# Modulation tiles add into one PSUM bank through zero-padded conditions, and the two gate tiles of the latent projections become one

## The chip, the cores and the metric

The kernel runs on one core of one Trainium2 chip. The metric is the device time of one launch in microseconds, the median of three runs. All arithmetic is in float32. The host only lays the inputs out.

## The reference

Two transformer blocks over 256 latent tokens of width 1024, with 256 memory or context tokens beside them. The first block mixes three attentions and a feed-forward layer of 16384 small experts, of which every token gathers 128 rows. The second block has two layers, an mLSTM mixer and a retention mixer, each followed by 16 experts of three 1024 x 1024 matrices with 32 tokens each. What the change touches is the modulation: two condition vectors (one for the latent tokens, one for the context) go through SiLU and, for each layer, a 1024 x 6144 matrix, and give shifts, scales and gates for every channel:

```python
def modulate(h, shift, scale):
    return h * (1 + scale) + shift

g = p[..., 2 * nq + 2 * nv:].astype(f32)
ig = g[..., :2 * A_HEADS].reshape(bn, t, 2, A_HEADS) + ig_b.astype(f32)
lf = jax.nn.log_sigmoid(g[..., 2 * A_HEADS:].reshape(bn, t, 2, A_HEADS) + fg_b.astype(f32))
```

The second part gives the mLSTM's 16 input gates and 16 forget gates per token, from the last 32 columns of its input matrix.

## The kernel before, in words

The program is a row of stages; within one, each engine has its own list of instructions, and at the end of each block of lists all engines wait for one another. Weights come by SyncE's DMAs of 2 MB each into a ring of six places (`issue`, line 257); a place is loaded again when the matmuls that read it are done (`k.release`). The order in each list is written out by hand.

**Modulations** (class at line 553). The two matrices make 24 tiles of 512 columns. For a tile, `tensor` (line 604) multiplies the two condition columns (`k.cond`, stationary, 2 columns for each of 8 chunks of 128 channels) with the 512 columns of the weights: the 8 products go to four groups of partitions (0, 32, 64, 96) of one PSUM bank, two into each, so rows 0 and 1 of each group hold partial sums. ScalarE copies the whole bank to SBUF (`scalar`, line 569, L574). `turn_rows` (line 594, L600) then multiplies each 128 columns of the copy (stationary) with `k.pick[:, 0:2]`, which adds the four groups and puts the channels on partitions. `tensor` begins with the turn of the tile before it. Once all tiles of a span are turned, VectorE adds the bias (`vector_end`, L589). Tiles 0 to 3 run beside the peer experts, 4 to 12 in the latent scan (`latent_scan`, between the 16 units of the scan), 13 to 15 in the norm ahead of the retention's projections, 16 to 18 in the retention heads, 19 to 21 ahead of the retention's output, 22 and 23 in the norm ahead of the second layer's experts.

**Latent projections** (`latent_scan`, run by `gemm`, line 450). The tile list begins with two tiles of 16 output rows, input and forget gates, each with its 8 chunks, then 8 tiles of queries and keys and 8 of values and outputs. ScalarE empties each into SBUF and adds the gates' bias (L2066).

**Latent scan.** For each of 16 units (8 heads, 2 directions) PE makes row maxima (L1512) and, once a head, scores (L1505), VectorE the exponents (L1552), ScalarE the exponential (L1530), GpSimd the mask (L1540), VectorE the weights (L1562), PE the output (L1524), VectorE its normalisation.

**Experts** (`experts`, line 2367). Ten places of 2 MB hold expert weights: the six of the ring and four more (`WeightsAhead.load`, line 2362, L2363), filled before the experts begin. After routing, GpSimd gathers the token rows of the first experts by an indirect DMA (`fetch_rows`, L2424), and PE turns them (L2592) and begins (L2584). Every place freed is loaded again (L2547). The last of the four extra loads waits in SyncE's list until the router's matmuls (L2445) have read the buffer it overwrites.

Of the kernel before, what the change touches and what calls it, by code (L numbers as in the profile page):

```python
# [19 lines left out]
ALU = mybir.AluOpType  # L20
# [3 lines left out]
P = 128  # L24
# [12 lines left out]
NEG = -1e30  # L37
ROOT_K, ROOT_A, ROOT_B = 0.3752449290315803, -3.335382431293894, 5.000310737319491
# [81 lines left out]
class Tile:  # L120


    def __init__(self, pairs, n, load, m, row, dst, gate, bias, s, c, needs):
# [16 lines left out]
def setup(nc, ctx, dram):  # L140
# [159 lines left out]
def constants(k):  # L300
# [7 lines left out]
    with nc.Block(no_gpsimd_drain=True) as block:  # L308
# [7 lines left out]
        def _(pool):  # L316
# [15 lines left out]
            st(pool, pool.tensor_tensor(k.pick[:], k.ident[:, 0:EXPERTS], k.ident[:, 32:32 + EXPERTS], ALU.add))  # L332
            st(pool, pool.tensor_tensor(k.pick[:], k.pick[:], k.ident[:, 64:64 + EXPERTS], ALU.add))
            st(pool, pool.tensor_tensor(k.pick[:], k.pick[:], k.ident[:, 96:96 + EXPERTS], ALU.add))
# [115 lines left out]
def gemm(k, name, tiles, evac, upto, engine="act", banks=4, beside=None, between=None, behind=None,  # L450
# [29 lines left out]
    with nc.Block(no_gpsimd_drain=True) as block:  # L480
        @block.tensor
        def _(pe):
            seen = None
            for i, t in enumerate(tiles):
# [7 lines left out]
                for j, (lhsT, rhs) in enumerate(t.pairs):  # L492
                    last = pe.matmul(bank(i), lhsT, rhs, start=(j == 0), stop=(j == len(t.pairs) - 1))  # L493
# [44 lines left out]
def tile(pairs, n, load=None, m=P, row=0, dst=None, gate=None, bias=None, s=None, c=None, needs=None):  # L538
    return Tile(pairs, n, load, m, row, dst, gate, bias, s, c, needs)
# [13 lines left out]
class Modulations:  # L553
# [7 lines left out]
    def __init__(self, k, at, first, last, banks, turned):  # L561

        self.k, self.first, self.last, self.banks, self.out = k, first, last, banks, turned
        self.sc, self.pick = k.cond[:], k.pick[:, 0:2]
# [15 lines left out]
    def vector_end(self, dve, first=None, last=None):  # L580
        k = self.k
        first, last = first or self.first, last or self.last
        dve.wait_ge(self.turned, last - self.first)
        for layer in range(2):
            n0, n1 = (4 * min(max(a - 12 * layer, 0), 12) for a in (first, last))
            if n0 < n1:
                at = 2 * (48 * layer + n0 - 4 * self.first)
                bias = k.col("ada_b")[:, 48 * layer + n0:48 * layer + n1]
                k.step_v.after(dve, dve.tensor_tensor(  # L589
# [14 lines left out]
    def tensor(self, pe, a, follows=True):  # L604
# [4 lines left out]
        elif follows:  # L609
            self.turn_rows(pe, a - 1)  # L610
# [2576 lines left out]
```

## Time and profile before

| | us |
|---|---|
| median of 3 runs | 2859.63 |
| lowest and highest | 2857.07, 2861.63 |
| profiled execution, own time | 2877.04 |
| its span, first to last instruction | 2875.3 |
| PE matmul busy | 2171.1 (76%) |
| VectorE busy | 1336.9 (46%) |
| GpSimd busy | 809.1 (28%) |
| ScalarE busy | 434.5 (15%) |
| moved by DMA | 976.00 MB, mean 339 GB/s |

The busy shares are averages over stages with different limits: peer experts until 1326 us, latent norm, projections and scan to 1514, output to 1590, first layer's experts to 2086, retention to 2365, second layer's experts to 2865. A row of the timeline gives the start, the time from the first to the last of merged instructions, the engine (PEld is PE's weight load, SPq and POOLq are lists of SyncE and GpSimd), the line, the operation, the operands and the count; in brackets stands how long the engine was idle before and what ended that. One float32 product appears as two matmul records.

### The profile page before, as it was taken

The numbers are of one execution on the slowest core, as the hardware profiler recorded it, in microseconds if no ns is written. First come the engines' busy times: TensorE is split into PE (matmuls) and PEld (weight loads), VectorE is DVE, ScalarE is ACT, GpSimd is POOL, SyncE is SP. The second block draws the span as 40 slices with busy tenths as digits, with TensorE's granted clock in tenths as the row PEclk, the third lists the DMA queues.
The fourth block names the chain that finished last, engine by engine and source line by source line (L and its number), as shares of the span: only waits on it lengthen the run. The fifth ranks groups of instructions, "written<-read, shape, count | busy, mean of one in ns | idle before, by whom it ended". The sixth has DMA issues, their size and how long they took to land. (4 is left out here: it accounts for less than half of the span.)

```text
span 2875.3 us, 26014 instructions
## 1 busy us (share of the span) xinstructions
PE 2171.1 (76%) x9844; PEld 1057.4 (37%) x9844; DVE 1336.9 (46%) x2870; ACT 434.5 (15%) x932; POOL 809.1 (28%) x902
## 2 busy tenths in 40 slices
PE   8976897868747656657999699988889986655554
PEld 5544344725312222224574233322245553222222
DVE  3578344979996777774483222112231332101011
ACT  1332100112210211102122210001021221000000
POOL 3335433458777777772010000000000000000000
PEclk9985898979978777788999899999999997788887
DMA  9989999899999999996564799999962469999997
GB/s 364 401 293 370 404 409 346 313 358 393 376 363 367 381 347 368 362 399 247 187 215 160 291 409 409 409 409 409 405 248 88 142 242 364 409 409 409 409 409 287
DMA packets 297103, 976.00 MB, mean 339 GB/s; under 512 B 22673, under 2 KB 23825, under 8 KB 296849
## 3 DMA queue, kind: packets, MB, share of 16 engines
q1 hardware_dynamic: 182770, 562.20, 50.5%
q0 software_dynamic: 114208, 412.14, 37.8%
q8 instruction: 78, 1.28, 0.2%
q14 instruction: 47, 0.39, 0.0%
HBM read 902.97 MB, written 71.30 MB: 339 GB/s over the span
## 5 line engine op out<-in xcount | busy, mean ns | idle before, releaser
L2584 PE MATMUL ps<-big 128*32 128x256 f32 (+1 forms) x4608 | 585.8, 517 | 210.6 <-DMA big<-in_moe_w_up_dram 78.7
L493 PE MATMUL ps<-big 128*128 128x512 f32 (+3 forms) x1648 | 543.5, 490 | 25.7 <-ACT big L2016 7.9
L1942 PE MATMUL ps<-big 128*128 128x512 f32 x512 | 326.0, 779 | 212.1 <-ACT big L1960 100.7
L2584 PEld LDWEIGHTS ps<-big 128*32 128x32 f32 (+1 forms) x4608 | 219.9, 133 | 557.4 <-issue 261.1
L493 PEld LDWEIGHTS ps<-big 128*128 128x128 f32 (+1 forms) x1648 | 306.0, 193 | 249.0 <-issue 218.4
L1994 DVE SCALAR_TENSOR_TENSOR big<-big 128x1024 f32<-128x1024 f32 x256 | 313.6, 1226 | 97.9 <-DMA big<-peer_rows,big 82.4
L1893 POOL DMA_INDIRECT big<-in_peer_v_dram,big x256 | 297.5, 1162 | 129.8 <-issue 73.2
L1886 POOL DMA_INDIRECT big<-peer_rows,big x256 | 282.5, 1103 | 98.9 <-issue 75.0
L1942 PEld LDWEIGHTS ps<-big 128*128 128x128 f32 x512 | 114.8, 242 | 387.7 <-issue 259.4
L2696 DVE TENSOR_TENSOR big<-big,ps 128x512 f32<-128x512 f32 (+1 forms) x32 | 17.8, 555 | 471.7 <-issue 452.1
L659 POOL DMA_DIRECT2D peer_rows<-big x256 | 149.6, 592 | 288.6 <-DVE big L671 288.2
L671 DVE STREAM_TRANSPOSE big<-big 128x1024 f32<-128x1024 f32 x128 | 150.7, 1220 | 104.9 <-DMA big<-in_peer_u_t_dram 104.2
L2677 DVE TENSOR_TENSOR big<-ps,big 32x256 f32<-32x256 f32 (+1 forms) x96 | 48.9, 510 | 270.7 <-PE ps L2584 268.7
L2424 POOL DMA_INDIRECT big<-m_rows,small x12 | 11.5, 956 | 575.8 <-PE ps L2592 539.9
L1982 DVE SCALAR_TENSOR_TENSOR big<-big 128x1024 f32<-128x1024 f32 x128 | 164.1, 1282 | 14.4 <-DMA big<-in_peer_v_dram,big 12.9
L2652 ACT ACTIVATE big<-ps 128x512 f32<-128x512 f32 (+1 forms) x32 | 15.7, 490 | 552.4 <-PE ps L2584 552.4
L2625 PE MATMUL ps<-big 128*128 128x512 f32 x160 | 83.2, 660 | 19.7 <-DVE big L2677 19.7
L1716 PE MATMUL ps<-big 128*128 128x512 f32 (+2 forms) x288 | 92.9, 476 | 0.0
L1154 PE MATMUL ps<-big 128*128 128x512 f32 x192 | 87.1, 607 | 5.9 <-PEq L480 5.9
L1524 PE MATMUL ps<-big 128*128 128x129 f32 x320 | 50.3, 311 | 43.8 <-DVE big L1562 25.1
L429 POOL DMA_DIRECT2D m_rows<-big x2 | 1.2, 576 | 259.5 <-DVE big L368 259.4
L616 PE MATMUL ps<-big,cond 128*2 128x512 f32 x384 | 52.9, 674 | 26.4 <-DMA big<-in_ada_w_dram 18.0
(378 smaller groups left out, 2032.7 us busy)
## 6 DMA issues: line engine op xcount, KB each, us to landing
big<-in_moe_w_gate_dram SPq DMA_DIRECT2D x64, 2048.0 KB, 24.0
big<-in_moe_w_up_dram SPq DMA_DIRECT2D x64, 2048.0 KB, 24.0
big<-in_moe_w_down_dram SPq DMA_DIRECT2D x64, 2048.0 KB, 24.0
big<-in_peer_u_t_dram POOLq DMA_DIRECT2D x64, 1024.0 KB, 14.0
peer_rows<-big POOLq DMA_DIRECT2D x256, 256.0 KB, 8.5
big<-in_ada_w_dram SPq DMA_DIRECT2D x24, 2048.0 KB, 8.0
big<-in_mlstm_w_in_dram SPq DMA_DIRECT2D x12, 2048.0 KB, 15.4
big<-in_w_in_dram SPq DMA_DIRECT2D x8, 2048.0 KB, 19.6
```

What stands on the lines that cost most here:

```text
L493: last = pe.matmul(bank(i), lhsT, rhs, start=(j == 0), stop=(j == len(t.pairs) - 1))
L659: pool.dma_start(self.out[q][:, 8 * m:8 * m + 8], self.dst[m % self.OUT][32 * q:32 * q + 32] .rearrange("p j i c w -> p (j i) (c w)")).the ...
L671: dve.transpose(self.dst[m % self.OUT][:, j].rearrange("p i c w -> p c i w"), self.src[m % self.IN][:, j])\
L1154: pe.matmul(k.ps[:, i % 4, :], k.ht[:, c, t * P:(t + 1) * P], w[:, c, :], start=(c == 0), stop=False)
L1716: last = pe.matmul(self.bank(i), lhsT, rhs, start=(j == 0), stop=(j == len(t.pairs) - 1))
L1886: pool.indirect_dma_start(out=u_buf[n % NU], out_offset=None, in_=rows.rows, in_offset=bass.IndirectOffsetOnAxis(ap=index_of(0, n), axis=0))\
L1893: pool.indirect_dma_start(out=v_buf[n % NV], out_offset=None, in_=values, in_offset=bass.IndirectOffsetOnAxis(ap=index_of(1, n), axis=0))\
L1942: last = pe.matmul(k.ps[:, 4 + 2 * t + half, :], diag[n // 2 % 4], v_buf[n % NV][:, 512 * half:512 * half + 512], start=(n < PER and n % G ...
L1982: dve.scalar_tensor_tensor(out=x, in0=v_buf[n % NV], scalar=w[:, n:n + 1], in1=x, op0=ALU.mult, op1=ALU.add)\
L1994: dve.scalar_tensor_tensor(out=u, in0=u, scalar=1.0, in1=h2[:, t].rearrange("p q c w -> p (q c w)"), op0=ALU.mult, op1=ALU.mult, accum_out ...
L2584: last = pe.matmul(k.ps[q * M:q * M + M, bank, 0:W], lhsT(kc), w4[i % RING][:, c, q * W:q * W + W], start=(kc == 0), stop=(kc == C - 1), s ...
L2625: pe.matmul(k.ps[:, 4 + j % 2, :], wb[:, t * P:(t + 1) * P], ys[:, 512 * nh:512 * nh + 512], start=True, stop=True).then_inc(c_full, 1)
```

## The change

Three edits. **Groups of modulation tiles.** `k.cond_at` holds, for each of 8 chunks, 34 columns of zeros with the two conditions in columns 16 and 17. A window of 2n columns that starts at 16 - 2i puts the conditions in columns 2i and 2i + 1 and zeros elsewhere, so tile i of a group of n adds its two rows to the bank and zeros to the other rows. ScalarE copies the bank and PE turns it once for each group. The groups are tiles 4 to 12, 13 to 15, 16 to 18, 19 to 21, and 22 with 23; tiles 0 to 3 stay alone. **Gate tiles.** One tile whose 16 products go alternately to partitions 0 and 32 of one bank; both ScalarE copies follow it. **Experts.** For the second layer the last extra load waits until the first gather has landed, instead of for the router's matmuls.

```diff
-    k.pick = sb("pick", [P, EXPERTS])
+    k.pick = sb("pick", [P, 32])
     k.cond = sb("cond", [P, 2 * C])
+    k.cond_at = sb("cond_at", [P, C * WIDE])
...
                 for j, (lhsT, rhs) in enumerate(t.pairs):
-                    last = pe.matmul(bank(i), lhsT, rhs, start=(j == 0), stop=(j == len(t.pairs) - 1))
+                    row = 32 * (j % t.groups)
+                    last = pe.matmul(bank(i) if t.groups == 1 else k.ps[row:row + t.m, i % banks, 0:t.n], lhsT, rhs,
+                                     start=(j < t.groups), stop=(j >= len(t.pairs) - t.groups),
+                                     skip_group_check=t.groups > 1)
...
     def scalar(self, act, a):
-        i = a - self.first
-        act.wait_ge(self.full, i + 1)
-        if i >= 2:
-            act.wait_ge(self.turned, i - 1)
-        act.activation(self.res[i % 2], self.k.ps[:, self.banks[i % len(self.banks)], :], ACT.Copy).then_inc(self.kept, 1)
+        g = self.group_of[a]
+        if a != self.groups[g][-1]:
+            return
+        act.wait_ge(self.full, a - self.first + 1)
+        if g >= 2:
+            act.wait_ge(self.turned, g - 1)
+        act.activation(self.res[g % 2], self.k.ps[:, self.banks[g % len(self.banks)], :], ACT.Copy).then_inc(self.kept, 1)
...
     def turn_rows(self, pe, a):
-        i = a - self.first
-        pe.wait_ge(self.kept, i + 1)
+        g = self.group_of[a]
+        tiles = self.groups[g]
+        at, n = 8 * (tiles[0] - self.first), len(tiles)
+        pe.wait_ge(self.kept, g + 1)
         for b in range(4):
-            at = 2 * (4 * i + b)
-            last = pe.matmul(self.out[:, at:at + 2], self.res[i % 2][:, b * P:(b + 1) * P], self.pick,
-                             start=True, stop=True)
+            last = pe.matmul(self.out[:, at + 2 * n * b:at + 2 * n * b + 2 * n], self.res[g % 2][:, b * P:(b + 1) * P],
+                             self.k.pick[:, 0:2 * n], start=True, stop=True)
         last.then_inc(self.turned, 1)
...
     def tensor(self, pe, a, follows=True):
-        i = a - self.first
+        g = self.group_of[a]
+        tiles = self.groups[g]
+        i, width = a - tiles[0], 2 * len(tiles)
         if i == 0:
-            pe.wait_ge(self.done, len(self.banks))
-        elif follows:
-            self.turn_rows(pe, a - 1)
+            if g == 0:
+                pe.wait_ge(self.done, len(self.banks))
+            elif follows:
+                self.turn_rows(pe, a - 1)
...
-            last = pe.matmul(k.ps[q:q + 2, self.banks[i % len(self.banks)], :], self.sc[:, 2 * c:2 * c + 2], w[:, c, :],
-                             start=(c < 4), stop=(c >= 4), skip_group_check=True)
+            last = pe.matmul(k.ps[q:q + width, self.banks[g % len(self.banks)], :],
+                             self.sc[:, c, WIDE_AT - 2 * i:WIDE_AT - 2 * i + width], w[:, c, :],
+                             start=(i == 0 and c < 4), stop=(i == len(tiles) - 1 and c >= 4), skip_group_check=True)
...
+        k.step_v.after(dve, dve.memset(k.cond_at[:], 0.0))
         k.step_v.after(dve, dve.tensor_tensor(k.cond[:], k.cond[:], k.col("cvec"), ALU.mult))
+        k.step_v.after(dve, dve.tensor_copy(
+            k.cond_at[:].rearrange("p (c w) -> p c w", w=WIDE)[:, :, WIDE_AT:WIDE_AT + 2],
+            k.cond[:].rearrange("p (c s) -> p c s", s=2)))
...
-    for a in range(2):
-        tiles.append(tile([(w[:, c, 16 * a:16 * a + 16], ht[:, c, :]) for c in range(C)], T, g0, m=16,
-                          dst=(scan.ig, scan.fg)[a], bias=k.col(("ig_b", "fg_b")[a])[0:16, :]))
+    tiles.append(tile([(w[:, c, 16 * a:16 * a + 16], ht[:, c, :]) for c in range(C) for a in range(2)], T, g0, m=16,
+                      groups=2))
...
         if t.m == 16:
-            return eng.activation(t.dst, ps, ACT.Identity, bias=t.bias)
+            eng.activation(scan.ig, ps, ACT.Identity, bias=k.col("ig_b")[0:16, :])
+            return eng.activation(scan.fg, k.ps[32:48, 0, 0:T], ACT.Identity, bias=k.col("fg_b")[0:16, :])
...
                 if s == X - 1:
-                    sp.wait_ge(by_expert, 1)
+                    sp.wait_ge(*((by_expert, 1) if S > 1 else (gathered, 16)))
                 ahead.load(sp, s)
```

`vector_end` now adds the bias in one instruction for each group and layer, from the order in which a group's turn leaves the channels; beside the peer experts these are four instructions, and they were one. `k.pick` grows from 16 to 32 columns.

## Rows read from the trace of the kernel before

**Rows 1.** The page: what DMA moved in 40 equal slices of the span.

```profile
GB/s 364 401 293 370 404 409 346 313 358 393 376 363 367 381 347 368 362 399 247 187 215 160 291 409 409 409 409 409 405 248 88 142 242 364 409 409 409 409 409 287
```

**Rows 2.** Windows: length, busy of PE, PEld, DVE, ACT, POOL, PEclk, DMA share, GB/s.

```profile
1347.00:1430.00 83.00, 82.96 (x260) 48.41 (x258) 36.28 (x112) 17.38 (x33) 0.00 (x0) 1.00 0.48 170
1451.39:1460.69 9.30, 9.30 (x65) 6.49 (x64) 7.86 (x29) 2.38 (x3) 2.52 (x6) 1.00 0.65 228
...
2289.30:2304.50 15.20, 15.20 (x121) 11.71 (x120) 8.57 (x16) 6.71 (x23) 0.00 (x0) 1.00 0.95 336
...
2366.00:2396.00 30.00, 11.63 (x94) 6.83 (x86) 13.92 (x50) 6.80 (x16) 2.14 (x3) 0.72 1.02 394
...
2410.00:2850.00 440.00, 257.29 (x2990) 117.67 (x2990) 45.45 (x105) 15.76 (x43) 1.89 (x2) 0.82 1.02 408
```

**Rows 3.** Timeline of the gate tiles: start, length, engine, line, operation, idle before.

```profile
1337.91 14.35 PE L493 MATMUL ps<-big 128*16 128x256 f32 x57 [3.21 <-PEq L351]
...
1343.24 0.46 ACT L2066 ACTIVATE big<-ps,cols 16x256 f32<-16x256 f32 x1 [8.37 <-PE ps L493]
...
1346.70 0.46 ACT L2066 ACTIVATE big<-ps,cols 16x256 f32<-16x256 f32 x1 [2.99 <-PE ps L493]
```

**Rows 4.** Timeline within a pair of scan units.

```profile
1453.06 0.95 PE L600 MATMUL ps<-pick,big 128*128 128x2 f32 x8
...
1453.94 1.90 PE L616 MATMUL ps<-big,cond 128*2 128x512 f32 x16
...
1458.78 1.99 PE L1505 MATMUL ps<-big 64*128 64x256 f32 x8
...
1460.86 1.28 DVE L1562 TENSOR_TENSOR big<-big,ps 128x256 f32<-128x256 f32 x4 [1.14 <-POOL big L1540]
```

**Rows 5.** Weight loads (ns min/median/max) by line, and the router's matmuls in the timeline.

```profile
L616 PEld LDWEIGHTS ps<-big,cond x384: 80/84/129, 588.4 to 2370.2; 128*2 128x2 f32 x192
...
L2445 PEld LDWEIGHTS ps<-big x32: 92/98/150, 1589.8 to 2376.7; 128*16 128x16 f32 x32
...
2376.26 1.06 PE L2445 MATMUL ps<-big 128*16 128x256 f32 x16 [1.12 <-PEq L351]
```

**Rows 6.** Timeline of the norm before the retention's projections.

```profile
2092.53 3.58 PE L616 MATMUL ps<-big,cond 128*2 128x512 f32 x16 [6.40 <-DVE ps L578]
...
2096.18 0.60 ACT L574 ACTIVATE big<-ps 128x512 f32<-128x512 f32 x1 [2.18 <-PE ps L616]
...
2099.78 0.60 ACT L574 ACTIVATE big<-ps 128x512 f32<-128x512 f32 x1 [3.00 <-PE ps L616]
...
2105.12 0.18 DVE L589 TENSOR_TENSOR mod<-ps,cols 128x24 f32<-128x24 f32 x1 [5.70 <-PE ps L600]
```

**Rows 7.** Timeline: the first matmuls of the retention's output.

```profile
2335.97 9.28 PE L3009 MATMUL ps<-big 128*128 128x512 f32 x21 [1.02 <-ACT big L3024]
```

**Rows 8.** Timeline: norm, last extra load, gather, and start of the second experts.

```profile
2369.09 1.42 DVE L368 TENSOR_SCALAR big<-big,small 128x1024 f32<-128x1024 f32 x2
...
2372.87 2.27 PE L401 MATMUL ps<-ident,big 128*128 128x128 f32 x16
...
2380.90 0.37 SPq L2363 DMA_DIRECT2D big<-in_moe_w_up_dram  x1
...
2388.34 0.99 POOL L2424 DMA_INDIRECT big<-m_rows,small  x1 [16.96 <-POOLq L2429]
2396.43 1.97 PE L2592 MATMUL ps<-ident,big 128*128 128x128 f32 x8 [14.20 <-DMA big<-m_rows,small]
...
2403.48 2.09 SPq L2547 DMA_DIRECT2D big<-in_moe_w_down_dram  x2
```

**Rows 9.** The twelve gathers of expert rows, line 2424.

```profile
DMA to landing us min/median/max: 4.3/7.6/8.8
```

**Rows 10.** Timeline: VectorE behind the conditions and behind the peer's bias addition.

```profile
56.32 2.37 DVE L671 STREAM_TRANSPOSE big<-big 128x1024 f32<-128x1024 f32 x2 [5.39 <-DMA big<-in_peer_u_t_dram]
...
643.87 1.23 DVE L1994 SCALAR_TENSOR_TENSOR big<-big 128x1024 f32<-128x1024 f32 x1 [1.99 <-DMA big<-peer_rows,big]
```

More of the change, by code:

```diff
@@ L37 @@
 NEG = -1e30
+WIDE, WIDE_AT = 34, 16
 ROOT_K, ROOT_A, ROOT_B = 0.3752449290315803, -3.335382431293894, 5.000310737319491
@@ L120, with __init__ @@
 class Tile:
-    def __init__(self, pairs, n, load, m, row, dst, gate, bias, s, c, needs):
+    def __init__(self, pairs, n, load, m, row, dst, gate, bias, s, c, needs, groups):
+        self.groups = groups
         self.pairs, self.n, self.load, self.m, self.row = pairs, n, load, m, row
@@ L535, in gemm, with tile @@
     full.base, free.base = full.base + len(tiles), free.base + len(tiles)
-def tile(pairs, n, load=None, m=P, row=0, dst=None, gate=None, bias=None, s=None, c=None, needs=None):
-    return Tile(pairs, n, load, m, row, dst, gate, bias, s, c, needs)
+def tile(pairs, n, load=None, m=P, row=0, dst=None, gate=None, bias=None, s=None, c=None, needs=None, groups=1):
+    return Tile(pairs, n, load, m, row, dst, gate, bias, s, c, needs, groups)
 def weights(k, n, step):
@@ L559, with __init__ @@
     TILES = 24
-    def __init__(self, k, at, first, last, banks, turned):
+    def __init__(self, k, at, first, last, banks, turned, groups=None):
         self.k, self.first, self.last, self.banks, self.out = k, first, last, banks, turned
-        self.sc, self.pick = k.cond[:], k.pick[:, 0:2]
+        self.groups = groups or [range(a, a + 1) for a in range(first, last)]
+        self.group_of = {a: g for g, tiles in enumerate(self.groups) for a in tiles}
+        self.sc = k.cond_at[:].rearrange("p (c w) -> p c w", w=WIDE)
         self.res = [work(k, at + 18 + 512 * j, 512) for j in range(2)]
@@ L2072, in latent_scan @@
     out = k.ps[:, 7, 0:64]
-    DECAYS, COLUMNS = 14, 15
-    mods = Modulations(k, 20992, FIRST_MODS, BESIDE_UNITS, (5,), k.ps[:, 7, :])
+    DECAYS, COLUMNS = 13, 14
+    mods = Modulations(k, 20992, FIRST_MODS, BESIDE_UNITS, (5,), k.ps[:, 7, :], [range(FIRST_MODS, BESIDE_UNITS)])
     def logs_and_silus(act, i, stored):
-        if i == 1:
-            stored(act, 1)
+        if i == 0:
+            stored(act, 0)
             scan.scalar_logs(act)
-        if 0 <= i - 3 < C:
-            scan.scalar_silu(act, i - 3)
+        if 0 <= i - 2 < C:
+            scan.scalar_silu(act, i - 2)
         if i == DECAYS:
@@ L2099, in convolve @@
         for c in range(C):
-            stored(dve, 2 + c)
+            stored(dve, 1 + c)
             scan.vector_conv(dve, c)
@@ L2451, in _ @@
                     at, j = (TT * s + t) * P, 16 * (S * t + s)
-                    last = pe.matmul(k.ps[:, 0, j:j + 16], logits_t[:, at:at + P], k.pick[:],
+                    last = pe.matmul(k.ps[:, 0, j:j + 16], logits_t[:, at:at + P], k.pick[:, 0:EXPERTS],
                                      start=True, stop=True)
```

36 lines of the change are left out of this document (21 added, 15 removed).

## The prediction

> **What bounds the kernel now.** I read the windows first, then the timeline at each of the four places where modulation tiles run, then the page's bandwidth line and the DMA landings. The span has two kinds of stretch. In the second expert stage the 16 DMA engines move 408 GB/s and are busy all the time while PE is busy 58% of it [rows 2]; the page's line shows the same plateau in the first expert stage [rows 1]. Such a stretch keeps its length, since its bytes are fixed, but it starts when PE frees the first ring place, so every microsecond taken off before it moves its end. Between the expert stages PE is the bound: it is busy 82.96 of 83 us in the latent projections, and 9.30 of 9.30 us in a pair of scan units and 15.20 of 15.20 us in the retention heads [rows 2], with DMA at 48% to 95%. So the question for each removed PE instruction is whether it stands in such a PE stretch, and for each removed wait what is late next. The profiled execution took 2877.04 us, its span 2875.3 us; the median of the runs is 2859.63 us, 17.4 us less. I take savings in the profile as savings of the median, since the parts concerned are a few microseconds each.
>
> **A. Input and forget columns in one pass.** Before, two tiles of 8 chunks. PE starts the first at 1337.91 at the low clock, and ScalarE copies it at 1343.24 and the second at 1346.70: the second costs 3.46 us at full clock [rows 3]. Now 16 products go alternately to partitions 0 and 32. Whether two such run at once is shown only for neighbours: the router's 16 matmul records (8 products of 256 columns, 16 stationary columns, four partition groups) take 1.06 us [rows 5], against 3.44 us for 8 products in one group. With two groups I expect 8 pairs in the time of 8 products, 3.44 us, so one tile goes. Bounds: 0 (no overlap) to 3.46. I take 3.3. ScalarE's two copies now follow one another at the end of the first tile, earlier than before; PE has four banks and isn't held. The rest of the projections is PE without idle time, so the 3.3 us reach its end.
>
> **B. Latent scan, 9 tiles in one group.** Between two tiles PE did a turn: 8 records from 1453.06, and the next tile's matmuls at 1453.94, so 0.88 us [rows 4]. Eight of nine turns go: 8 x 0.88 = 7.0 us. What is late next: a pair of units with one tile takes 9.30 us; VectorE is busy 7.86 us of it [rows 2], and waits for the scores of PE line 1505, 1458.78 to 1460.8, before its L1562 at 1460.86 [rows 4]. PE's pair becomes 8.42 us, above 7.86 by 0.56, so PE stays the bound, narrowly. ScalarE loses eight copies and their waits, which stood ahead of its exponentials. Bounds: 0, if VectorE's gaps between instructions fill the pair, to 7.0. I take 6.7, for the start and end of the scan where the two alternate.
>
> **C. Norm before the retention input, 3 tiles.** The cycle is tile, copy, turn, tile: from the copy at 2096.18 to the next at 2099.78 it takes 3.60 us, and the last turn lets VectorE add at 2105.12 [rows 6]; a tile's matmuls alone take 1.90 us [rows 4]. Nothing else is late: the loads for the input are there, and the rows were normalised before. Now: first tile to 2096.1 as before (3.58 us, low clock), two more at 1.90, copy, turn: VectorE adds at about 2101.8. That is 2 x (3.60 - 1.90) = 3.4; I take 3.3, with bounds 2 (if the transposes behind then wait for something) and 3.4.
>
> **D. Retention heads, 3 tiles.** Two turns go, in a stretch where PE has no gap [rows 2]: 2 x 0.88 = 1.8 us, bounds 0 and 1.8.
>
> **E. Retention output, 3 tiles.** The same cycle as C stands ahead of the transposes, so 2 x 1.70 = 3.4 us. The output matmuls wait 1.02 us for ScalarE's L3024 [rows 7], which follows the transposes and moves with them. I take 3.3, bounds 2 and 3.4.
>
> **F. Second expert stage's norm, and the last early load.** Two tiles: one cycle fewer, 1.7 us, before PE's L401 at 2372.87 [rows 8]. Rows are normalised at 2370.5, so 1.6 us of it counts. The gather of the expert rows is issued at 2388.34 and PE starts on it at 2396.43; an early load of 2 MB was issued at 2380.90, and DMA is saturated over the whole stretch (share 1.02, 394 GB/s) [rows 2, 8]. That load is 5.1 us of DMA at 409 GB/s. SyncE now issues it when the gather has landed. The twelve gathers land in 4.3 us at best, 7.6 in the middle, when DMA is full [rows 9]. The rest of the backlog ends near 2396.4 - 5.1 = 2391.3. So the gather, issued at 2386.7, lands between 2391.0 (4.3) and 2394.3 (7.6); I take 2392.0, 4.4 us earlier. Against it: SyncE's wait stands before the end of the block, so all engines now pass that edge after the landing: one DMA issue (0.37 us) and an edge, which at L2445 left PE idle 1.12 us, part of it from other causes [rows 5]; I take 0.9 together. Behind SyncE only this load is queued. The load takes DMA to about 2397.5; PE frees its first place at 2403.48 now [rows 8] and near 2400.0 then, so the load fits into the idle window and nothing is added to the saturated stretch. F = 4.4 - 0.9 = 3.5, bounds -3.5 (gather no faster than the 1.6 us, and the load adds its 5.1 us) and 5.
>
> A rule speaks against F. The Trainium skill, DMA: Bandwidth & Descriptors, section on queues, rings and completion order, says that each DMA engine takes turns packet by packet between the queues that have work. By it the gather, which has its own queue, would wait little behind SyncE's loads, and holding one back would give little (half a megabyte at half rate instead of full, 1.3 us more), so the sum would be that of rival 1. The 8.1 us from issue to PE's start against 4.3 in an idle machine [rows 8, 9] do not agree with it in size; it is a rival below.
>
> **G. What is added.** A memset of 272 columns and a copy of 16 on VectorE at the first projections, and four additions instead of one beside the peer experts, 0.2 us each. VectorE waits 5.39 us for DMA soon after the first, and 1.99 us directly behind the additions [rows 10]; both are hidden, at most 1 us without that cover. The stationary operand grows from 2 to up to 18 columns: its load takes 84 ns at 2 and 98 ns at 16 [rows 5] and lies beside the matmuls. GpSimd's wider pick is some nanoseconds at the start. I count 0.
>
> **Sum.** 3.3 + 6.7 + 3.3 + 1.8 + 3.3 + 3.5 = 21.9 us. The profiled execution would take 2855.1 us, the median 2859.6 - 21.9 = 2837.7 us.
>
> **Rivals.** (1) *The gather isn't bound by the backlog*, or only by as much as it shares: half a megabyte at half of 409 GB/s takes 1.3 us more than at all of it, so F is 1.6 - 0.9 = 0.7 plus at most 1.3, total 19.1 to 20.4, 2840 us. For it: the slowest of twelve gathers took 8.8 us [rows 9] although the machine was full for far longer than that, so none waits for all that is queued. Against it: 8.1 us here against 4.3 at best. The worse form, where the load also lengthens the saturated stretch, gives F = -3.5 and 2844.7 us.
> (2) *VectorE becomes the bound of the scan*. With its 29 instructions and their gaps it may need 8.9 us for a pair: B is 0.4 x 8 = 3.2, total 18.4, 2841 us. For it: 7.86 busy of 8.42 leaves little.
> (3) *The two partition groups don't overlap* in the gate tile, so the change doesn't do there what it says: A = 0, total 18.6, 2841 us. For it: no row shows two groups. Against it: four groups do overlap.
> (4) *Slower: the padded tiles lose their overlap.* A modulation tile is 8 products in four groups, 1.90 us now, where 8 serial ones would take twice the 3.46 us of 8 products of 256 columns, 6.9 us [rows 3, 4]. If up to 18 stationary columns made neighbours wait for weights, each of the 20 grouped tiles would grow. At twofold overlap it costs 20 x 1.55 = 31 us more, the time would be 2859.6 - 21.9 + 31 = 2869 us. It turns the sign from 21.9 / 20 = 1.1 us a tile on, a tile of 3.0 us. Against it: 16 columns in four groups ran 256-column products in 1.06 us [rows 5], half of a tile's 512.
>
> **Chances.** The forecast, all six parts within their sizes (2834 to 2840.5): 0.62. Rival 1: 0.14. Rival 2: 0.08. Rival 3: 0.06. Two of 1 to 3 together: 0.03. Rival 4: 0.04, of which 0.03 slower and 0.01 still no change. No change otherwise, from waits that I don't see: 0.03. The range 2832 to 2849 leaves out rival 4 and the last case, 0.07, and about 0.08 of the tails of the others. A difference under 0.2% (5.7 us) can't be told from no change here. Faster 0.93, same 0.04, slower 0.03.
>
> **What would show it.** A: one tile of 32 matmul records from line 493's place, 3.4 us from the first ScalarE copy of gates to the next copy gone. B: a pair of scan units of 8.4 us, with VectorE idle under 0.6 us; one turn at the end. C, E: tiles 1.90 us apart with no copy between. D: pairs of heads shorter by 0.88. F: gather landing within 5.5 us of its issue, and the first freed place 3 to 4 us earlier relative to PE's L401. Wrong would be: a tile of over 2.2 us, a longer saturated stretch (more than its bytes over 409 GB/s), PE waiting for the load held back, or a new PE wait for VectorE in the scan.

## The result, and the profile after

The changed kernel takes 2843.3 us (median of 6 runs, 2831.97 to 2847.89) against 2859.06 us for the kernel before (6 runs). The medians are 15.8 us apart; estimated from all runs the ratio is 0.9938, 95% interval 0.9916 to 0.996, so 17.7 us less, between 11.4 and 24.0. Forecast were 21.9 us less, 2837.7 us, range 2832 to 2849. The profiled execution took 2846.36 us, its span 2844.6.

The spans of the two profiles differ by 30.7 us, which is more than the runs do. The table divides each profile at the start of PE's first matmul of a stage (the retention output and the second experts end with the last one); behind each of the two kernels stands its second profile, taken for the experiments below.

| stretch | before | again | changed | again | saved (first pair) | forecast |
|---|---|---|---|---|---|---|
| peer stage, up to the gate tile | 1337.9 | 1340.2 | 1329.6 | 1316.5 | 8.3 | - |
| A latent projections | 93.17 | 94.42 | 89.73 | 90.30 | 3.4 | 3.3 |
| B latent scan | 88.65 | 93.26 | 83.37 | 83.40 | 5.3 | 6.7 |
| its output, first experts | 572.8 | 572.7 | 572.1 | 572.3 | 0.7 | 0 |
| C norm before the retention input | 17.74 | 17.68 | 13.72 | 13.65 | 4.0 | 3.3 |
| retention input | 169.70 | 169.70 | 169.71 | 169.71 | 0.0 | 0 |
| D retention heads | 40.56 | 40.56 | 39.01 | 39.00 | 1.6 | 1.8 |
| E retention output, up to the transposes | 11.66 | 11.66 | 9.04 | 9.00 | 2.6 | 3.3 |
| rest of the output | 31.50 | 31.51 | 31.51 | 31.50 | 0.0 | 0 |
| F second norm, up to its transposes | 9.17 | 9.16 | 8.96 | 8.96 | 0.2 | - |
| F to the gather's issue | 15.47 | 15.46 | 15.25 | 15.26 | 0.2 | - |
| F issue to PE's start | 8.08 | 8.07 | 6.14 | 6.26 | 1.9 | all of F: 3.5 |
| second experts | 459.6 | 460.6 | 460.0 | 460.6 | -0.3 | 0 |
| end | 19.23 | 16.51 | 16.53 | 17.73 | 2.7 | 0 |

A to F sum to 19.3 us, inside the interval of the runs. In the second pair they sum to 24.4 us, 9.9 of it in B, whose length has two values (see the kernel before again, below). The rest of the 30.7 us is the peer stage, which lies between 1310.8 and 1345.8 us over all profiles here, and the end. The profiles come from several chips, on which the kernel before had medians from 2855.9 to 2878.8 us, so part of that range is the chip's. No effect of the change on the peer stage is visible; a small one isn't excluded.

**Gate tile.** Timeline of the changed kernel (columns as in [rows 3]):

```profile
1329.59 10.70 PE L497 MATMUL ps<-big 128*16 128x256 f32 x56 [2.85 <-PEq L354]
...
1334.95 0.47 ACT L2088 ACTIVATE big<-ps,cols 16x256 f32<-16x256 f32 x1 [8.03 <-PE ps L497]
1335.43 0.47 ACT L2089 ACTIVATE big<-ps,cols 16x256 f32<-16x256 f32 x1
```

The copy comes 5.36 us after PE's start, where 8 products alone took 5.33 [rows 3]: 16 products in two partition groups take the time of 8. The second copy follows the first. Over the ten profiles with the merged tile the projections take 89.4 to 91.0 us, over the three with two tiles 93.0 to 94.4.

**Scan.** Two pairs of units in the windows (columns as in [rows 2]), then the one place near the scan's end where PE waits:

```profile
1441.57:1450.10 8.53, 8.53 (x57) 5.65 (x56) 8.19 (x30) 1.90 (x2) 1.82 (x4) 1.00 0.70 245
1433.05:1441.57 8.52, 8.52 (x57) 5.64 (x56) 8.18 (x30) 1.90 (x2) 1.83 (x4) 1.00 0.65 233
```

```profile
1479.98 1.91 PE L634 MATMUL ps<-big,cond_at 128*18 128x512 f32 x16
1482.42 1.99 PE L1528 MATMUL ps<-big 64*128 64x256 f32 x8 [0.52 <-DVE big L1585]
```

PE is still busy all the time, but a pair is 8.53 us and not 8.42, and VectorE is busy 8.19 of it. A tile with an 18-column stationary takes 1.91 us, with 2 columns 1.90 [rows 4].

**Norm before the retention input** (answers to [rows 6]):

```profile
2074.78 6.75 PE L634 MATMUL ps<-big,cond_at 128*6 128x512 f32 x48 [6.48 <-DVE ps L588]
...
2081.61 0.60 ACT L584 ACTIVATE big<-ps 128x512 f32<-128x512 f32 x1 [5.34 <-PE ps L634]
...
2083.36 0.18 DVE L603 TENSOR_TENSOR mod<-ps,cols 128x24 f32<-128x24 f32 x1 [1.67 <-PE ps L615]
```

Three tiles run without a copy between them; 8.58 us from the first product to VectorE's addition, and 12.59 in [rows 6]. The clock has a part in it. Windows of the changed kernel's tiles, then one of the first tile before:

```profile
2074.78:2077.60 2.82, 2.82 (x16) 0.57 (x20) 2.68 (x7) 1.49 (x4) 0.00 (x0) 0.50 1.05 386
2077.80:2081.50 3.70, 3.70 (x36) 0.69 (x28) 3.49 (x10) 0.00 (x0) 0.00 (x0) 1.00 1.05 386
```

```profile
2092.53:2095.90 3.37, 3.37 (x16) 0.40 (x16) 3.13 (x9) 1.48 (x4) 0.00 (x0) 0.50 1.05 388
```

The granted clock (seventh column) rose 2.9 us after the first product, and 3.4 us after it before.

**Retention output, second norm, gather** (timeline; the last answers to [rows 8]):

```profile
2299.08 7.24 PE L634 MATMUL ps<-big,cond_at 128*6 128x512 f32 x48
...
2339.78 5.31 PE L634 MATMUL ps<-big,cond_at 128*4 128x512 f32 x32 [2.02 <-PEq L3010]
...
2346.72 2.27 PE L404 MATMUL ps<-ident,big 128*128 128x128 f32 x16
...
2361.98 0.99 POOL L2447 DMA_INDIRECT big<-m_rows,small  x1 [16.56 <-DVEq L2452]
2367.24 0.37 SPq L2386 DMA_DIRECT2D big<-in_moe_w_up_dram  x1
...
2368.12 1.94 PE L2615 MATMUL ps<-ident,big 128*128 128x128 f32 x8 [12.37 <-PEq L2452]
...
2375.05 2.10 SPq L2570 DMA_DIRECT2D big<-in_moe_w_down_dram  x2
```

Three tiles take 7.24 us and two take 5.31, where 5.7 and 3.8 were expected. The granted clock says why. Windows of the changed kernel:

```profile
2297.20:2303.20 6.00, 5.99 (x32) 2.33 (x36) 4.29 (x16) 1.09 (x2) 0.00 (x0) 0.52 0.82 291
2339.80:2343.80 4.00, 4.00 (x24) 0.90 (x28) 3.62 (x15) 1.10 (x2) 0.00 (x0) 0.59 0.99 397
```

and of the kernel before, in the same work:

```profile
2321.70:2332.00 10.30, 8.85 (x65) 2.97 (x64) 3.14 (x12) 2.28 (x4) 0.00 (x0) 0.86 0.97 377
2365.70:2371.30 5.60, 4.78 (x40) 1.63 (x40) 4.86 (x16) 1.75 (x3) 1.07 (x2) 1.00 1.03 366
```

Clocks of 0.52 and 0.59 are mostly the 1.2 GHz level; such a stretch is called a dip below. Before, the second norm's two tiles ran at 2.4 GHz throughout.

The saturated stretch is as before in all but its start: 408 GB/s, share 1.02 (compare [rows 2]).

```profile
2374.00:2814.00 440.00, 267.30 (x3034) 121.45 (x3026) 45.41 (x105) 16.14 (x43) 1.89 (x2) 0.80 1.02 408
```

### The profile page after: what moved, and what is told of

Read it like the earlier page. It is cut to its first block and busy times, and to the rows that moved or that the text cites. A ratio compares the mean times of both kernels' runs of the same rounds, so it can differ in the third digit from the quotient of the medians.

```text
span 2844.6 us, 25750 instructions
## 1 busy us (share of the span) xinstructions
PE 2165.8 (76%) x9724; PEld 1046.2 (37%) x9724; DVE 1339.9 (47%) x2875; ACT 427.1 (15%) x917; POOL 830.2 (29%) x902
## 5 line engine op out<-in xcount | busy, mean ns | idle before, releaser
L497 PE MATMUL ps<-big 128*128 128x512 f32 (+3 forms) x1648 | 535.6, 488 | 17.2 <-PEq L354 6.5
L1916 POOL DMA_INDIRECT big<-in_peer_v_dram,big x256 | 309.9, 1211 | 102.2 <-issue 68.0
L1909 POOL DMA_INDIRECT big<-peer_rows,big x256 | 290.6, 1135 | 98.9 <-issue 75.0
L2719 DVE TENSOR_TENSOR big<-big,ps 128x512 f32<-128x512 f32 (+1 forms) x32 | 17.7, 554 | 464.2 <-issue 445.2
L634 PE MATMUL ps<-big,cond_at 128*6 128x512 f32 (+3 forms) x384 | 55.1, 709 | 25.8 <-DMA big<-in_ada_w_dram 17.3
```

What stands on the lines that cost most here:

```text
L497: last = pe.matmul(bank(i) if t.groups == 1 else k.ps[row:row + t.m, i % banks, 0:t.n], lhsT, rhs, start=(j < t.groups), stop=(j >= len(t. ...
L1909: pool.indirect_dma_start(out=u_buf[n % NU], out_offset=None, in_=rows.rows, in_offset=bass.IndirectOffsetOnAxis(ap=index_of(0, n), axis=0))\
L1916: pool.indirect_dma_start(out=v_buf[n % NV], out_offset=None, in_=values, in_offset=bass.IndirectOffsetOnAxis(ap=index_of(1, n), axis=0))\
```

## The experiments

**The same two kernels again.** No edit.

> The changed kernel once more, with nothing altered, for a narrower interval and a second profile. Theory 1 (stages): the change saves 19 to 22 us from the first gate tile on; then the ratio to the kernel before is 0.9925 to 0.9935, and the 15.8 us between the medians so far is the scatter of the peer stage ahead of it. Rival (the change costs something in the peer stage, from the four additions in place of one or the wide stationary operand): the ratio stays at 0.9945 and the first gate tile starts some 5 us later than the kernel before's. Clock: in the first profile the first modulation tile of the retention input took 2.95 us instead of 3.58, those of the retention output met a low clock of 6 us where there were 3 before, and the two of the second expert norm took 5.31 us instead of 3.8. If these dips fall by chance, they lie elsewhere in this profile and the stages C, E and F move by 0.5 to 1.5 us; if they belong to the program, they lie at the same places.

Measured: 2838.34 us (6 runs), ratio 0.9938 [0.9915, 0.9961]. The ratio lies between the two that were expected, and its interval holds both, so it doesn't decide. The changed stages repeat to 0.1 us, the projections but for 0.6, and the dips of the clock lie where they did. The gate tile starts 21 us earlier than in the kernel before and 13 earlier than in the first profile; that speaks against a cost in the peer stage, though other chips may have a part in it.

> The kernel before, unaltered, for a second profile. Stage theory: the stages that the change touches repeat to 0.1 us (latent projections 93.2 us, scan 83.4 us and its wait, norm before the retention input 17.7, retention output up to PE's transposes 11.7, second norm 9.2, gather issue to PE's start 8.1), and the peer stage ahead of them does not: 1337.9 us in the first profile, 1310 to 1340 in the others. Rival: the first profile of the kernel before was out of the ordinary in these stages too, and part of the 19.3 us that I read there is chance.

Measured: one run of 2883.29 us. C to F repeat to 0.1 us. A and B don't: the projections have 1.3 us more and the scan 4.6 us more; in the scan it is the low clock at its start (the scores of PE line 1505 at 3.78 us instead of 1.99). Over the runs with grouped tiles the scan has 82.7 to 83.4 us (five profiles) or 86.7 to 86.9 us (five) in the same way: that stretch has two lengths in both kernels. Compared long with long, B saves 6.3 to 6.5 us, and short with short 5.3 to 5.9.

**Gate tiles as two again.**

```diff
-    tiles.append(tile([... for c in range(C) for a in range(2)], T, g0, m=16, groups=2))
+    for a in range(2):
+        tiles.append(tile([... for c in range(C)], T, g0, m=16, dst=(scan.ig, scan.fg)[a], ...))
```

> The changed kernel with two gate tiles of 8 products each, as before. If two partition groups overlap fully, the latent projections from the first gate matmul to the first scan matmul take 3.4 us more than the 89.74 us of the changed kernel: 93.1 us. If they overlap only in part and the rest of the gain came from elsewhere (ScalarE's earlier copies, a clock dip that ended earlier), less than 3 us. Total 3.4 us more in the first case.

Measured: ratio 0.9941 [0.9918, 0.9964], an interval too wide for 3.4 us; the projections take 93.01 us, 3.3 and 2.7 more than in the two profiles of the changed kernel. Timeline of this kernel:

```profile
1330.32 0.47 ACT L2089 ACTIVATE big<-ps,cols 16x256 f32<-16x256 f32 x1 [8.00 <-PE ps L497]
1333.77 0.47 ACT L2089 ACTIVATE big<-ps,cols 16x256 f32<-16x256 f32 x1 [2.99 <-PE ps L497]
```

The copies stand 3.45 us apart again. Two groups overlap fully.

**Groups of one.**

```diff
-        self.groups = groups or [range(a, a + 1) for a in range(first, last)]
+        self.groups = [range(a, a + 1) for a in range(first, last)]
```

> The changed kernel with every group of modulation tiles cut to one tile, so each is copied and turned for itself again; gate tile and gathered wait stay. Theory 1: a pair of scan units takes 9.30 us again instead of 8.53, the scan 5.2 us more in all, the norm before the retention input 3.4 to 4.0 us more, retention heads and output 4.2 us more, the second expert norm 0.2 to 1.7 us more; total 13 to 15 us more. Rival (the grouping as such matters less, VectorE was nearly the bound of the scan): scan less than 4 us longer, with VectorE waits in place of the turns. If the price of a turn in the scan is 0.88 us as I read it before, the pairs differ by 0.88; the changed kernel's trace says 0.77, since the matmul in front of a tile then runs 0.09 us longer.

Measured: 2851.73 us, ratio 0.9986 [0.9967, 1.0005], where the changed kernel had 0.9938 on the same chip: 13.7 us of the 17.7 are gone. Scan 88.82 us (5.4 more), norm 18.10 (4.4), heads 40.56 (1.6), output 11.66 (2.6), second norm 9.15 and its issue (0.4); the gather gets 1.0 us faster. Sum 13.4. Timeline in the scan of this kernel:

```profile
1429.82 1.83 PE L1547 MATMUL ps<-big 128*128 128x129 f32 x14
1431.49 0.95 PE L615 MATMUL ps<-pick,big 128*128 128x2 f32 x8
1432.37 1.90 PE L634 MATMUL ps<-big,cond_at 128*2 128x512 f32 x16
...
1439.12 1.83 PE L1547 MATMUL ps<-big 128*128 128x129 f32 x14
1440.79 0.95 PE L615 MATMUL ps<-pick,big 128*128 128x2 f32 x8
```

A turn starts 1.67 us after the products in front of it, a tile in its place 1.76 us after them (the same line in the changed kernel: 1439.81 to 1441.57). A turn therefore costs 0.88 - 0.09 = 0.79 us there, not 0.88.

**All windows 32 columns wide.**

```diff
-WIDE, WIDE_AT = 34, 16
+WIDE, WIDE_AT = 48, 16
...
-        i, width = a - tiles[0], 2 * len(tiles)
+        i, width = a - tiles[0], 32
```

> The changed kernel with every modulation tile's stationary window 32 columns wide, the whole partition group, whatever the group's size (2, 4, 6 or 18 columns before). My rival 4 said that more stationary columns could cost the overlap of the four partition groups. In the changed kernel 18 columns take 592 ns a record and 1.91 us a tile, 2 columns 591 to 593 ns and 1.90 us. If width costs nothing up to the group, a tile stays at 1.90 to 1.95 us and every stage keeps its length, pair of scan units 8.53 us. If there is a step above 18 columns (rival), a tile takes over 2.2 us and the scan 2.7 us more in all. The weight load grows from 94 ns to some 100 to 110 ns and stays beside the matmuls.

Measured: ratio 0.9931 [0.991, 0.9952]. All records of the tiles in this kernel (weight loads, then matmuls):

```profile
L634 PEld LDWEIGHTS ps<-big,cond_at x384: 106/110/178, 587.8 to 2364.1; 128*32 128x32 f32 x192
L634 PE MATMUL ps<-big,cond_at x384: 589/592/1063, 587.8 to 2364.5; 128*32 128x512 f32 x192
```

A load takes 110 ns instead of 84 to 94, a tile 1.92 us. Zeros up to the whole partition group cost 0.01 to 0.02 us a tile. Not every stage kept its length: C has 15.24 us, E 7.90 and the scan its longer value, by dips in other places. The second norm had no dip and took 7.28 us instead of 8.96, but PE began on the gathered rows 30.3 us after the end of the retention output, and 30.4 us after it in the changed kernel. Timeline of this kernel's norm and gather:

```profile
2361.46 3.64 PE L634 MATMUL ps<-big,cond_at 128*32 128x512 f32 x32 [2.02 <-PEq L3010]
...
2381.99 0.99 POOL L2447 DMA_INDIRECT big<-m_rows,small  x1 [14.89 <-DVEq L2452]
...
2389.73 1.94 PE L2615 MATMUL ps<-ident,big 128*128 128x128 f32 x8 [14.69 <-PEq L2452]
```

The norm's 1.7 us went into a longer gather.

**The early load waits for the router again.**

```diff
-                    sp.wait_ge(*((by_expert, 1) if S > 1 else (gathered, 16)))
+                    sp.wait_ge(by_expert, 1)
```

> The changed kernel, but the last early load of the second experts waits for the router's matmuls again and not for the gather. Backlog theory (the gather queues behind all that was issued before it): gather from issue to landing 8.0 us instead of 5.2, PE begins on it right after the landing, so 2.0 us later than in the changed kernel; total 2 us more. Sharing rival (each DMA engine takes turns between queues): landing within 6.5 us of the issue, and PE begins no later than in the changed kernel, since 0.9 us of block edge goes; total within 0.7 us, or less time. In both the stretch from PE's first expert matmul to the last stays 459.6 to 460.0 us, since the held load fits into the idle time of DMA.

Measured: ratio 0.9943 [0.9923, 0.9962], which separates nothing; issue to PE's start 8.08 us instead of 6.14 and 6.26. The second experts take 458.8 us, less than the 459.6 to 460.0 expected and 1.2 to 1.8 less than in the changed kernel, so most of the 1.9 us at the gather isn't seen behind them: from the end of the retention output to PE's last expert matmul it is 491.1 us here and 490.9 in the next kernel, and with the load held 490.3 and 491.1 (changed kernel) and 491.1 (gate tiles as two). The last load of weights landed 1.5 to 2.1 us earlier with the load held; why PE's end doesn't follow it stays open. Timeline:

```profile
2349.02 0.99 POOL L2447 DMA_INDIRECT big<-m_rows,small  x1 [16.57 <-POOLq L2452]
...
2357.10 1.97 PE L2615 MATMUL ps<-ident,big 128*128 128x128 f32 x8 [14.39 <-DMA big<-m_rows,small]
```

**The early load issued together with the gather.**

```diff
-                    sp.wait_ge(*((by_expert, 1) if S > 1 else (gathered, 16)))
+                    sp.wait_ge(*((by_expert, 1) if S > 1 else (indexed, P // N)))
```

> The changed kernel, but the last early load of the second experts waits until the row numbers are ready, so it is issued at the same time as the gather and not after its landing. Backlog theory (what is issued first moves first, each in its queue and the engines by order of issue): the gather lands 5.2 to 5.5 us after its issue as in the changed kernel, the edge after the landing goes, and PE begins 5.3 us after the issue instead of 6.2. Sharing rival (the engines take turns between queues with work): the gather's half megabyte shares with the load, and its landing comes up to 1.3 us later, 6.5 us after the issue. The kernel with the old wait, where the load was issued 7 us before the gather, had 8.0 us.

Measured: ratio 0.9934 [0.991, 0.9959].

```profile
2372.45 0.37 SPq L2386 DMA_DIRECT2D big<-in_moe_w_up_dram  x1
...
2381.22 1.97 PE L2615 MATMUL ps<-ident,big 128*128 128x128 f32 x8 [14.51 <-DMA big<-m_rows,small]
```

The gather (issued 2373.12) takes 8.05 us, as with the load 7 us ahead of it. Neither theory had that. The landings in the traces show more, and so do the records of single DMA packets, of which the third column is taken (from the gather's issue to the start of its first packet). The last column counts the gather's landing from the end of the retention output.

| kernel | issue | first packet | last ring load landed | gather landed | early load landed | issue to landing | from retention output |
|---|---|---|---|---|---|---|---|
| before | 2388.34 | 4.22 | 2390.86 | 2396.38 | 2397.92 | 8.04 | 32.7 |
| wait for the router | 2349.02 | 4.21 | 2352.82 | 2357.05 | 2359.11 | 8.03 | 32.3 |
| issued with the gather | 2373.12 | 4.20 | 2377.11 | 2381.17 | 2383.41 | 8.05 | 32.3 |
| changed | 2361.98 | 1.85 | 2365.93 | 2367.15 | after it | 5.17 | 29.4 |
| wait in the next block | 2371.30 | 1.69 | 2375.04 | 2376.27 | after it | 4.97 | 29.4 |
| groups of one | 2357.66 | 1.73 | 2360.60 | 2361.85 | after it | 4.19 | 28.8 |
| windows of 32 | 2381.99 | 3.26 | 2388.45 | 2388.76 | after it | 6.77 | 29.3 |
| all together (below) | 2336.39 | 3.42 | 2342.59 | 2343.04 | after it | 6.65 | 29.2 |

The gather never waits for the early load to finish: it lands 1.5 to 2.2 us ahead of it. With that load next in SyncE's queue, no packet of the gather moves for 4.2 us while SyncE's queue moves over 400 GB/s; from then on the gather has half of the bytes (0.49 to 0.51). The other gathers of the kernel before do the same: of its twelve, the nine issued into full DMA have their first packet after 4.16 to 4.26 us and then 0.48 to 0.53 of the bytes, the three issued with DMA idle after 1.67 to 1.69 us. So the larger part of the 2.9 us between 8.04 and 5.17 stands ahead of the first packet, not in the sharing. With the load held, SyncE's queue runs low earlier, and the landing stands 28.8 to 29.4 us behind the retention output in every such kernel of the table, issued 22.5 us after it or 24.6: the backlog sets it, and a gather issued earlier takes longer. The Trainium skill, DMA: Bandwidth & Descriptors, section on queues, rings and completion order, lets each engine drain a whole packet of several descriptors from one queue before the next has its turn. The equal shares agree with turns; the 4.2 us ahead of the first packet don't follow from them, and their cause isn't shown here.

**SyncE's wait in the next block.**

```diff
@@ first block, sync
-                    sp.wait_ge(*((by_expert, 1) if S > 1 else (gathered, 16)))
+                    if S == 1:
+                        break
+                    sp.wait_ge(by_expert, 1)
@@ second block, sync
+            if S == 1:
+                sp.wait_ge(gathered, 16)
+                ahead.load(sp, X - 1)
```

> The changed kernel, but SyncE's wait for the gather and the last early load stand at the head of its list in the next block, so no engine has to pass a block edge after the gather's landing. If the 0.97 us from the gather's landing to PE's first transpose is that edge (it was 0.05 us in the kernel before), PE begins 0.1 us after the landing, and gather issue to PE's start is 5.3 us instead of 6.2; 0.9 us less in all. Rival: the edge costs nothing more, and the 0.97 us is the low clock or PE's own wait: no change, 6.1 to 6.3 us. The gather itself takes 5.2 to 5.3 us from issue to landing in both.

Measured: ratio 0.9927 [0.9901, 0.9954]; issue to PE's start 5.01 us, 1.1 and 1.2 less than in the changed kernel.

```profile
2371.30 0.99 POOL L2447 DMA_INDIRECT big<-m_rows,small  x1 [16.79 <-POOLq L2452]
...
2376.32 1.97 PE L2620 MATMUL ps<-ident,big 128*128 128x128 f32 x8 [11.13 <-DMA big<-m_rows,small]
```

PE starts 0.05 us after the landing: the 0.97 us were the block edge. Here the dips of the clock lay otherwise: C 15.25 us, E 7.89 us, as with the windows of 32. So they hold their places from run to run mostly, not always.

**PE kept busy at block edges.** Nothing reads what these matmuls write; they stand at the end of PE's list (9 after the retention heads, 5 after the retention output, 16 after the first experts).

```diff
+def warm(k, pe, n, bank):
+    for _ in range(n):
+        pe.matmul(k.ps[:, bank, 0:P], k.ident[:], k.ident[:], start=True, stop=True)
```

> The changed kernel with matmuls of the identity with itself at the end of PE's list in three blocks, where PE otherwise waits at the edge: 9 after the retention heads (PE idle 3.4 us there), 5 after the retention output (2.0 us), 16 after the first experts (6.5 us). Nothing reads their bank. Clock theory: the dips after these edges (6.2 us at 0.5 in the retention output, 4 us in the second expert norm, 1.2 us in the norm before the retention input) come from PE's idleness at the edge, and shrink or go. Then the retention output up to PE's transposes takes 7.5 us instead of 9.0, the second expert norm 7.5 instead of 8.96, and the norm before the retention input 13.2 instead of 13.7. Rival 1: the dips stay where they are, since PE's wait at the edge can't be filled fully; stages keep 9.0, 8.96 and 13.7 us. Rival 2: the added matmuls make PE arrive last at the edges, and the stages before them grow by up to 1 us each.

Measured: 2852.74 us against 2875.49, ratio 0.9907 [0.9877, 0.9936]. E takes 6.25 us instead of 9.04, the second norm 7.26 instead of 8.96, the stages ahead of the edges the same. C has 13.77 us as in the changed kernel: there the 16 matmuls shortened nothing. Of the 4.5 us gained, 1.1 go back at the gather (7.28 us from issue to PE's start): issued earlier, it has more of the backlog before it. The second experts take 461.8 us instead of 460.0 and 460.6, so the norm's 1.7 us isn't seen at PE's end, 491.6 us after the retention output. Windows of the same tiles:

```profile
2306.80:2312.00 5.20, 5.20 (x49) 1.19 (x48) 3.33 (x13) 1.08 (x2) 0.00 (x0) 1.00 0.99 339
2345.60:2349.20 3.60, 3.59 (x32) 0.78 (x32) 3.21 (x14) 1.14 (x2) 0.00 (x0) 1.00 0.99 383
```

The clock is 1.00 in both. PE stood idle 1.39 us ahead of the first (3.40 in the changed kernel) and 0.90 ahead of the second (2.02).

**PE kept busy before the gather lands**: 30 such matmuls ahead of PE's wait, on top of the moved wait.

> As the kernel with the wait in the next block, and PE runs 30 matmuls of the identity with itself (128 columns, into a PSUM bank that nothing reads, some 7.5 us at full clock) before it waits for the first gather of the second experts. In the changed kernel the granted clock is 0.5 from 2355 to 2374 us, where PE first stood idle for 12.4 us and then worked. Clock theory: the low clock follows the idleness, so with PE busy until shortly before the landing it stands at 1.0 when the expert's work begins; the stretch from the gather's landing to the first freed ring place, 7.9 us in the changed kernel (2367.15 to 2375.05), becomes 5 to 5.5 us, and the whole time falls by 2.5 us more than from the moved wait alone. Rival: the clock stays at 0.5 whatever PE did, and the stretch keeps its length, or the 30 matmuls at low clock run past the landing (15 us) and delay PE by up to 7 us.

Measured: ratio 0.9918 [0.9887, 0.9949].

```profile
2371.83 9.63 PE L2370 MATMUL ps<-ident 128*128 128x128 f32 x60 [6.38 <-PEq L2458]
2381.30 1.04 PE L2626 MATMUL ps<-ident,big 128*128 128x128 f32 x8
```

Both halves of the expectation came true at once: the work behind ran at full clock (8 records in 1.04 us instead of 1.94, and 4.5 us from there to the first freed place instead of 6.9), but the matmuls began at 0.50, ran past the landing at 2376.79 and held PE by 4.5 us.

**Everything together**, with counts set from these two.

```diff
+            warm(k, pe, 14, 0)
             turn_normed(3)
@@ end of the routing block
+            warm(k, pe, 16, 2)
@@ experts
+            warm(k, pe, 9 if S > 1 else 14, 5)
             turn_rows(0)
@@ end of the experts
+            if S > 1:
+                warm(k, pe, 22, 0)
@@ end of the retention heads, end of the retention output
+            warm(k, pe, 9, 0)
+            warm(k, pe, 5, 0)
```

> The changed kernel with the held load's wait in the next block, and matmuls of the identity (into a bank that nothing reads) wherever PE waits long enough: 9 and 5 at the ends of the retention heads and output, 22 at the end of the first experts, 14 ahead of the last four-row turn in the first scan's output, and ahead of each first gather 16 at the end of the routing block and then 9 (first layer) or 14 (second). From the run with 9 and 5: retention output up to PE's transposes 6.3 us instead of 9.0, second expert norm 7.3 instead of 9.0. From the run with 30: the stretch from PE's first transpose of gathered rows to the first freed place 4.5 us instead of 7.0; with 14 PE begins within 1 us of the landing, where 30 overran it by 4.5 us. Clock theory: first layer's stretch from the router's matmul to the first expert matmul 22 us instead of 24.4, since its matmuls no longer run at the low level; second layer: PE's norm transposes to the first freed place 26 us instead of 28.3. Sum against the changed kernel: 2.8 + 1.7 + 1.1 + 2 to 2.5 + 2 to 4, 10 to 12 us; ratio to the kernel before about 0.989 to 0.990. Rival: the earlier start of a saturated stretch gives nothing at its end, since DMA had other bytes to move; then the stage of the second experts grows by what was saved ahead of it, and the total gains only 4 to 6 us.

Measured: 2830.68 us (6 runs) against 2859.52, ratio 0.9901 [0.9882, 0.992]. The interval meets that of the changed kernel at its edge, so that it beats it is likely and not shown by the times alone; from the gate tile to the end its profile has 1506.9 us where the changed kernel has 1515.0 and 1517.6. C 12.29 us, E 6.25, second norm 7.26, first routing up to the first expert matmul 23.08 instead of 24.46. The gather gives some of it back again, 6.69 us, and the second experts keep their length (459.4 us), so the rival that the saturated stretch would grow isn't borne out. The sum expected was 10 to 12 us against the changed kernel; the profiles give 8.1 and 10.7. For the first routing 22 us were expected. For the second layer, from the norm's transposes to the first freed place, it was 26 us: it took 29.1, more than the changed kernel's 28.3. The matmuls there ended 3.2 us before the landing, and PE was at the low clock again:

```profile
2343.08 1.97 PE L2628 MATMUL ps<-ident,big 128*128 128x128 f32 x8 [3.17 <-DMA big<-m_rows,small]
```

## Why the prediction was right, and where its sizes were off

The direction, the range and the places were right: 19.3 us by the profile and 17.7 by the runs, of 21.9, and the removed turns and copies account for most of it. That the sum is so near is in part luck: the clock gave C 0.6 us and took 1.1 from E, and the runs can't tell 21.9 from rival 1's 19.1 to 20.4.

- **A** was right, 3.4 of 3.3, and undone alone it comes back. Rival 3 falls.
- **B**, 5.3 of 6.7. The term "8 x 0.88" was mis-sized: 0.88 is the distance from a turn's start to the tile's, but the turn overlaps the products in front of it by 0.09 us more than a tile does, and a pair gave 0.77 to 0.78. One of the eight turns gave next to nothing: PE now waits 0.52 us for VectorE there. So rival 2 holds in one place of eight, and one of the signs of being wrong, a new wait of PE for VectorE, came true at that size.
- **C**, 4.0 of 3.3, and **E**, 2.6 of 3.3: the chain of copies and turns went as worked out. The differences are the clock, which I had carried over unchanged. In C the clock rose 0.5 us sooner after the first product, inside the first tile, which is the same work in both kernels (6.75 us for three tiles; 3.58 + 3.8 were expected); why it rose sooner isn't shown. In E PE ran at the low level 3.4 us longer. Runs with the dips elsewhere have C at 15.2 and E at 7.9, which would be savings of 2.5 and 3.8 us.
- **D**, 1.6 of 1.8: two turns at 0.78.
- **F**, 2.4 of 3.5. The mis-sized term is the gather's landing, "4.4 us earlier": it came 3.3 us earlier, counted from the end of the retention output. The forecast took 2396.4 for the end of the whole backlog and subtracted the load's 5.1 us; but the gather had landed 1.5 us ahead of that load. That the backlog sets the landing was right, and so the norm's gain is no part of it: with the norm shorter by another 1.7 us the landing stayed. In the changed kernel that gain was 0.4 us instead of 1.6, since the two tiles met the low clock and took 5.31 us. Rival 1 had the mechanism, half shares, and too small a price: 1.3 us where 2.9 were measured, for want of the 4.2 us ahead of the first packet. Measured F lies nearer to its upper end, 2.0, than to 3.5. The 0.9 us for the edge were right (0.97, gone with the wait moved). That "every microsecond taken off before it moves its end" is not borne out for the held load: at the end of the second experts at most 0.8 us of its 1.9 are seen.
- **G** was right as far as the profiles tell: from the gate tile on no stage without a counted part grew by more than 0.4 us. The peer stage scatters too much to show its part.
- **Rival 4** falls: 1.91 us a tile at 18 columns, 1.92 at 32.

The totals alone could not have settled any part but the grouping: every interval is 10 us wide or more, and the single parts are 1.6 to 5.3 us.

## What to carry to other kernels

Partial results that fit side by side in one PSUM bank can be collected there by zero columns in the stationary operand, at a price of at most 0.02 us a tile up to the width of the partition group, and copied and turned once. Price a removed instruction by the difference of whole cycles with and without it, not by the distance to the next one's start, and read the granted clock of each short stage, since an edit that moves PE's pauses moves the low-clock stretches. An urgent small transfer lands sooner when the next large one is held back until it has landed, with the wait placed where no block edge hangs on it; look behind the next saturated stage whether the time is still saved there. If a backlog sets the landing, issuing the transfer earlier gains nothing.

## What the runs showed of the hardware

- PE fell to the 1.2 GHz level after a pause of 2.0 us (second norm, changed kernel) and not after a pause of 2.0 us in the same place in the kernel before and in the one with windows of 32; with idle time of 0.9 us there it stayed at 2.4 GHz. Filling pauses with unread matmuls shortened two stages of 9 us by 2.8 and 1.7 us and a third, C, not at all.
- A gather of 0.52 MB had its first packet 1.7 us after its issue with DMA idle, and 4.2 us after it with another queue full (404 to 411 GB/s); then it had half of the bytes. It didn't matter whether the other queue's next 2 MB were issued 0.7 or 7 us ahead of the gather.
- The peer stage varied by 35 us over the profiles (1310.8 to 1345.8, several chips), the first experts with their routing and output by 2.1 us, the second experts by 4.3, and the retention stages by 0.1 us but for the clock. What a small change does is read there, stage by stage.
